# Even layer of a four-layer forward pass: products in another order, recurrence operands made chunk by chunk, key norms by token, padded exponentials

## What is computed

```python
def even_mixer(xn, ...):
    proj = xn @ w_in                                  # 256 x 1024 @ 1024 x 2816
    lru_x, lru_g, rw = jnp.split(proj, [512, 1024], axis=-1)
    h = rg_lru(causal_dwconv(lru_x, conv_w, conv_b), gate_a_w, ...)
    y_lru = jax.nn.gelu(lru_g) * h
    y_rwkv = rwkv7_mixer(rw, shift_mu, ...)
    return jnp.concatenate([y_lru, y_rwkv], axis=-1) @ w_out

def rwkv7_mixer(p, mu, w0, w2, a0, a2, g2, k_k, k_a, r_k, gn_w, gn_b):
    ps = p + (token_shift(p) - p) * mu
    r, k, v, xw, xa, xg = jnp.split(ps, idx, axis=-1)    # 512, 512, 512, 64, 64, 128
    wlog = -jax.nn.softplus(-(w0 + jnp.tanh(xw) @ w2)) - 0.5
    decay = jnp.exp(-jnp.exp(wlog))
    a = jax.nn.sigmoid(a0 + xa @ a2)
    g = jax.nn.sigmoid(xg) @ g2
    kk = hs(k * k_k)                                     # 8 heads of 64
    kk = kk / jnp.maximum(jnp.linalg.norm(kk, axis=-1, keepdims=True), 1e-12)
    k = k * (1.0 + (a - 1.0) * k_a)
    o = rwkv7_scan(r, decay, k, v, kk, a)                # recurrence over the tokens
    ...                                                  # group norm, bonus of r, k, r_k, gate g
```

## Time and profile before

| | |
|---|---|
| time, median of 3 runs | 2103.97 us (2101.36 to 2104.2) |
| the profiled execution | 2104.11 us |
| its span in the trace | 2102.0 us |
| PE / DVE / ACT / POOL busy | 92% / 75% / 55% / 3% of the span |
| mean granted clock of TensorE | 0.919 |
| DMA | 489 MB, mean 233 GB/s |
| experts (336 tiles), the largest part | DVE low splits 750.8 us, ACT high splits 625.8 us |
| low and high splits outside the experts | x100 each, 219.1 and 183.6 us |

### The profile page before, as it was taken

The page is one execution under the profiler, slowest core; times in us unless marked ns, Lnnn a source line. Parts: engine busy times, 40 slices in busy tenths (PEclk is TensorE's granted clock), DMA queues, the critical chain, the costliest instruction groups (busy, mean ns, idle before and its releaser), DMA issues.

```text
span 2102.0 us, 25666 instructions
## 1 busy us (share of the span) xinstructions
PE 1923.9 (92%) x9324; PEld 1617.9 (77%) x9324; DVE 1583.2 (75%) x1546; ACT 1152.6 (55%) x1195; POOL 59.8 (3%) x85
## 2 busy tenths in 40 slices
PE   8748979999996799999999999999999998888987
PEld 7648867778784578888888888888888877677766
DVE  6587355788867478988888988888898886656754
ACT  5411214434436466777767676776777665454542
POOL 1000000111010000000000000000000000000000
PEclk9878659999996799999999999999999999959978
DMA  7300004899640379999999999999998973313420
GB/s 260 113 1 1 31 20 160 285 326 320 208 139 35 135 278 380 332 374 349 366 346 361 378 334 371 350 363 345 359 379 335 374 273 107 119 41 113 145 81 20
DMA packets 161947, 489.02 MB, mean 233 GB/s; under 512 B 8178, under 2 KB 13427, under 8 KB 161744
## 3 DMA queue, kind: packets, MB, share of 16 engines
q1 hardware_dynamic: 153536, 458.21, 60.0%
q0 software_dynamic: 8336, 29.81, 4.0%
HBM read 485.36 MB, written 2.62 MB: 232 GB/s over the span
## 4 chain that ended last, share of the span: by engine, by line
PE 67%; DVE 14%; issue 10%; DMA 4%; ACT 4%; POOL 0%; DVEq 0%; ACTq 0%; POOLq 0%
PE bank L1127 18%; PE bank L1129 18%; PE bank L1128 18%; DVE weights_at L1819 3%; PE bank L1305 2%; DMA BIG<-in_e_ffn_down 2%; ACT weights_at L2703 1%; PE bank L1553 1%; PE bank L1278 1%; DVE BIG L2120 1%; PE bank L1618 1%; DMA BIG<-in_e_ffn_gate 1%; PE bank L1266 1%; PE bank L1293 1%; DMA BIG<-in_w_ada 1%
## 5 line engine op out<-in xcount | busy, mean ns | idle before, releaser
L2361 DVE TENSOR_TENSOR expert_weights_low<-BIG,expert_weights_high 128x2048 fp32r<-128x2048 f32 x336 | 750.8, 2288 | 58.7 <-ACT expert_weights_high L2956 58.6
L2956 ACT ACTIVATE expert_weights_high<-BIG 128x2048 fp32r<-128x2048 f32 x336 | 625.8, 1922 | 69.3 <-DMA BIG<-in_o_moe_up 38.4
L1127 PE MATMUL bank<-expert_weights_high,expert_x_high 128*128 128x512 f32 x896 | 351.8, 393 | 3.0 <-DVE expert_x_low L2426 2.9
L1129 PE MATMUL bank<-expert_weights_low,expert_x_high 128*128 128x512 f32 x896 | 349.3, 390 | 0.0
L1128 PE MATMUL bank<-expert_weights_high,expert_x_low 128*128 128x512 f32 x896 | 349.1, 390 | 0.0
L1819 DVE TENSOR_TENSOR weights_at<-BIG,weights_at 128x2048 fp32r<-128x2048 f32 (+2 forms) x100 | 219.1, 2191 | 96.3 <-ACT weights_at L2703 94.4
L2703 ACT ACTIVATE weights_at<-BIG 128x2048 fp32r<-128x2048 f32 (+2 forms) x100 | 183.6, 1836 | 177.4 <-DMA BIG<-in_e_ffn_down 39.7
L1127 PE MATMUL bank<-weights_at,x_high 128*128 128x512 f32 (+2 forms) x608 | 244.9, 403 | 25.6 <-DVE weights_at L1819 11.9
L1128 PE MATMUL bank<-weights_at,x_low 128*128 128x512 f32 (+2 forms) x608 | 239.7, 394 | 0.0
L1129 PE MATMUL bank<-weights_at,x_high 128*128 128x512 f32 (+2 forms) x608 | 239.6, 394 | 0.0
L1127 PEld LDWEIGHTS bank<-expert_weights_high,expert_x_high 128*128 128x128 f32 x896 | 168.3, 188 | 37.3 <-DVE expert_x_low L2426 3.0
(11 more groups left out here) (398 smaller groups left out, 2436.4 us busy)
## 6 DMA issues: line engine op xcount, KB each, us to landing
BIG<-in_o_moe_gate SPq DMA_DIRECT2D x112, 1024.0 KB, 5.2
BIG<-in_o_moe_up SPq DMA_DIRECT2D x112, 1024.0 KB, 5.6
BIG<-in_o_moe_down SPq DMA_DIRECT2D x112, 1024.0 KB, 5.3
BIG<-in_w_ada POOLq DMA_DIRECT2D x48, 512.0 KB, 5.0
BIG<-in_w_in SPq DMA_DIRECT2D x20, 1024.0 KB, 5.0
BIG<-in_o_w_qkv SPq DMA_DIRECT2D x12, 1024.0 KB, 5.1
BIG<-in_e_w_in SPq DMA_DIRECT2D x10, 1024.0 KB, 5.4
BIG<-in_e_ffn_gate SPq DMA_DIRECT2D x10, 1024.0 KB, 6.2
```

The lines of the kernel that those rows point to most:

```text
L1127: mm(b, high_l, high_r, start=start, stop=False, skip_group_check=not check)
L1129: last = mm(b, high_l, low_r, start=False, stop=stop, skip_group_check=not check)
L2361: tt_(E_WL[q % E_SLOTS], half(q % E_SLOTS), E_WH[q % E_SLOTS].bitcast(F32), SUB).then_inc(w_low, 1)
L2956: f(E_WH[q % E_SLOTS], half(q % E_SLOTS), ACT.Copy).then_inc(w_high, 1)
```

## The change

Six things are done at once, all in the even layer ahead of the recurrence, and nothing in the code from its end on:

- The column chunks are loaded and multiplied in the order LRU input, LRU gate, lora, k, r, v. TensorE's program is written out, with the lora products inside chunk k, g and the key sums behind r, the key norms' spread inside v, LRU gates and bonus behind v, and only the by-token groups of v ahead of the masked products; the other four stand behind these.
- The token shift is made by chunk. ScalarE empties the bank with scale 1 - mu (`unshifted`), VectorE adds mu times the bank's neighbour column (`token_shift`, 128 x 255 per block); the buffer RW is gone.
- The key norms are summed by token (matmuls of 2 columns, `key_sums`), so that root and reciprocal work on 128 x 16, and are then spread over the channels by a copy and eight matmuls with the identity (`key_norms`).
- The exponentials lie in an array with one padded column per 64 tokens (`EPP`), of which the shifted and the unshifted one are two views: two exponentials instead of three, with the factor exp(-0.5) in their scale instead of in a VectorE pass.
- Squares, the mix of keys with a and all by-token copies are ScalarE's; silu of c, exp and sin of small arrays move behind the LRU sigmoids; `lambda_difference` moves into the last step of the recurrence (c == 3), with one `low()`.
- `low()` and `high()` stand at other places and, on VectorE, in another number.

The core of the diff (left out are the plan, the semaphores, the buffers' places and the bodies that only moved):

```diff
+W_IN_ORDER = [0, 1, 5, 3, 2, 4]
...
+        EPP = R(21024, 1040).rearrange("p (c k t) -> p c k t", c=4, t=HALF + 1)
+        EP, EPX = EPP[:, :, :, 1:HALF + 1], EPP[:, :, :, 0:HALF]
...
+            w_in(0, 0)
+            w_in(0, 1)
+            w_in(1, 0)
+            w_in(1, 1)
+            w_in(5, 0)
+            w_in(5, 1)
+            w_in(3, 0)
+            loras()
+            w_in(3, 1)
+            w_in(2, 0)
+            w_in(2, 1)
+            gates_g()
+            key_sums()
+            w_in(4, 0)
+            key_norms()
+            w_in(4, 1)
+            lru_gates()
+            bonuses()
+            pe.wait_ge(shifted, 4)
+            rows_by_token((4, 5))
             pe.wait_ge(chunk_ops, 1)
...
+            rows_by_token(range(4))
...
-            gemm(6, projections, 11)
-
-            wait_taken(v, ("w_in", 9))
-            V(tt_(PS, RW[:, :, 0:T], RW[:, :, 1:T + 1], SUB))
-            for c in range(CT_RW):
-                V(stt(PS[:, c, :], PS[:, c, :], prm("e_shift_mu", c), RW[:, c, 1:T + 1], MUL, ADD),
-                  shifted if c == CT_RW - 1 else None)
+            def token_shift(c):
+                units = w_in_units(c)
+                for u in units:
+                    b = take(v, ("w_in", u))
+                    scaled_units[0] += 1
+                    v.wait_ge(shift_scaled, scaled_units[0])
+                    for i in range(2):
+                        k = 2 * u - 8 + i
+                        V(stt(PS[:, k, 1:T], b[:, i * T:(i + 1) * T - 1], prm("e_shift_mu", k), PS[:, k, 1:T], MUL, ADD),
+                          ev if i else None)
+                v.sem_inc(shifted, 1)
+            def key_inverse_norms():
+                wait_taken(v, "key_sum")
+                V(ts(s_kn, s_kn, 1e-12, None, ALU.max))
+                V(d.reciprocal(s_kn, s_kn))
+                v.wait_ge(exps_ready, 2)
+                V(d.tensor_copy(v3(KX, 16), bc(s_kn, 2, [P, 16, HALF])), key_roots)
...
+            low()
+            rotations()
+            lambdas()
+            low()
+            softplus()
+            convolution(0)
+            convolution(1)
+            low()
+            convolution(2)
+            convolution(3)
+            low()
+            token_shift(5)
+            low()
+            decay_sums()
+            low()
+            token_shift(3)
+            v.wait_ge(exps_ready, 2)
+            V(tt_(KT, PS[:, 4:8, :], KT, MUL))
+            low()
+            token_shift(2)
+            key_inverse_norms()
+            bonus_products()
+            low()
+            chunk_operands()
+            low()
+            token_shift(4)
...
-            V(ts(KN, KN, 1e-12, None, ALU.max))
-            V(d.reciprocal(KN, KN))
-            V(tt_(KK, KK, KN, MUL))
...
+                elif c == 3:
+                    lambda_difference()
+                    low()
...
+            sigmoids("lora", (TMP, KB), ("e_w0", "e_a0"))
+            high()
+            for c in range(4):
+                A(f(KT[:, c, :], KB[:, c, :], ACT.Identity, scale=prm("e_k_a", c), bias=s_omka[:, c:c + 1]))
+            high()
+            act.wait_ge(cum_ready, 1)
+            per_chunk = CW.rearrange("p c (k t) -> p c k t", t=HALF)
+            A(f(EP, per_chunk, ACT.Exp, scale=-math.exp(-0.5)), exps_ready)
+            A(f(EN, CW, ACT.Exp, scale=math.exp(-0.5)), exps_ready)
+            unshifted(3)
+            high()
```

## The result

The changed kernel takes 2143.35 us (median of 4 runs, 2143.17 to 2143.51) against 2103.77 for the kernel before in the same comparison (2101.36 to 2104.2): a ratio of 1.0184, 95% interval 1.0171 to 1.0198. Forecast were 2124 us and a range up to 2136. The direction was right; the loss is 39.6 us instead of 20. The profiled execution took 2143.31 us with a span of 2141.5.

The account below looks back on a forecast made before the run. The even layer's preparation was taken as a chain between engines, the feed-forward as TensorE-bound. 2104 - 12 (earlier recurrence) + 32 (low splits one tile behind) = 2124 us, own spread 2110 to 2134, range 2097 to 2136.

Parts of the forecast that it names:

- 130': Start of the first recurrence product in the changed kernel (the mark ' means its times), instead of 142.25: a gain of 12.
- I take 3.5 of 0 to 6: First products: us lost to TensorE's lowered clock behind three new waits, where the rule alone gave 6.9.
- the first is nearly covered by ScalarE's exponentials: First products: the clock loss behind the 5.7 us wait is hidden by ScalarE's exponentials; only 0.6 shows.
- The lag as such: Behind the preparation: 13 low splits instead of 14 put each later place one tile behind; +32 us, bounds 24 and 42.
- The output product: From VectorE's end at 320.36 to tile 20's low split: late splits make TensorE wait, +10.5 us in sum.
- TensorE waits 2.3: Output product: TensorE waits 2.3 us for tile 13's low split, which now comes there, ending at 322.7'.
- D: Feed-forward: time of down-first's load, from the end of up-first's low split to ScalarE's high split; taken as 6.0.
- The turn: Feed-forward: a turn takes 34.4 + D = 40.4 us instead of 34.8; three turns cost +11.6.
- I take 6.0, bounds 5.0 and 8.0: Feed-forward: size of D; 5.0 when nothing else loads, 7.6 with an ada load just ahead.
- the upper row (7.6): Feed-forward: the profile's load time with an ada load just ahead; by the shared-engines rule 2 us more in four turns.
- The lag is not absorbed: Rival, lag absorbed in the feed-forward's turns: faster, 2104 - 15 + 7 = 2096; chance 0.15.
- The preparation gains nothing: Rival: clock stays at half through tiles 7 to 11, 15 more; 2104 + 3 + 32 = 2139; chance 0.07.

Follow-up runs that it names:

- experiment 1: Changed kernel with low(2) in place of low() in the recurrence's last step, so 14 low splits again: 2091.02 us, ratio 0.9934.
- experiment 3: Changed kernel with modulation loads of 64 columns instead of 1024 behind the first two steps: 2123.64 us, ratio 1.0071.
- experiment 8: Changed kernel with low(2) in the recurrence's last step and modulation loads of 64 columns: 2087.15 us, ratio 0.9923.
- experiment 9: Changed kernel with one low split more at the end of the feed-forward's first chunk: 2106.55 us, ratio 1.0007.
- experiment 2: Kernel before with one low split less in the first products (10 instead of 11 in that loop): 2150.92 us, ratio 1.0213.
- experiment 4: Kernel before with one low split moved from the first products into the recurrence's last step: 2097.76 us, ratio 0.9976.

## Why the prediction was right in kind and short in size

- **The preparation.** The waits were forecast at 5.7, 7.4 and 10.8 and are 6.8, 7.2 and 11.1; the first masked product was forecast at 130' and is at 133.46. What failed is the term "I take 3.5 of 0 to 6" for the clock. Four tiles stand behind a wait and each takes 1.7 to 1.9 us more (windows above), 7.3 in all. The wait of 3.3 ahead of tile 6 was in the sum with its length (46.8 to 50.2') and not with its clock, and "the first is nearly covered by ScalarE's exponentials" was wrong: the chain of waits of the changed kernel (start, us, what) goes from tile 7's product over k's last ScalarE passes, which wait for the product and not for the exponentials, to tile 9's low split.

```profile
76.58 0.48 ACT BIG L2834
...
77.69 0.49 DVE BIG L2016
...
80.11 2.30 DVE weights_at L1890
```

The page "TensorE: Matmul & The Clock Gate" of the Trainium skill ("What's actually happening") has the throttled state as the default, from which activity releases the engine. By that rule alone three waits stood at 6.9; the trace gives these three 5.6 and the fourth 1.7, which is nearer to the rule than to my discount. The mark itself is partly scatter and partly luck. The traces of experiments 1, 3, 8 and 9, with the same code up to there, have it at 131.1 to 131.9; they reach tile 7 at 66.7 to 67.4, this one at 68.92. And behind tile 7 the changed kernel needs 64.5 us where the forecast without clock had 61.4, though the clock took 5.6 there: other steps were priced some 2.5 us too long.
- **The lag as such.** That 13 low splits instead of 14 make all later places one tile late was right: experiments 1, 2 and 4 show it twice, at 52.3 and 53.2 us (48.5 by the stages of the two traces). The forecast was 32 (24 to 42): the term was mis-sized in all its parts, and this is what put the time outside the range.
- **The output product**, 14.6 instead of 10.5: "TensorE waits 2.3", 3.1 and 2.1 were right (1.95, 3.26, 2.20), but I let the product behind a wait take 5.6 us. It takes 7.35 (313.85 to 321.20) and 7.11 (324.49 to 331.60), 3 us together, and the next split waits for the sum of both. The same clock price that I had set for the preparation was left out here. Up to down-first of chunk 1's hidden values it is 7.0 instead of 5.1: D is 7.1 there (405.28 to 412.40) instead of 6.0, the rest was not taken apart.
- **The turn**, 43.1 instead of 40.4: the chain D + 34.4 was right and D was not. "I take 6.0, bounds 5.0 and 8.0" met 8.8, 7.3 and 7.2, on average 7.8, which makes 5.3 of the 8.2 us missed in three turns. I counted one modulation load ahead of it; two steps stand there (four issues of 512 KB). I set the upper row (7.6) aside because "the engines are less full". They are less full over the three turns (a DMA share of 0.76), but it is the loads issued just ahead that count. The main page of the Trainium skill, "Trainium Kernel Development and Optimization" ("Key Constraints"), has all queues on the same 16 engines. By that rule the higher row was the one to take, and the runs agree (experiment 3: 5.1, 5.0 and 5.1 without those loads). The other 2.9 us lie in the 34.4: from down-first to up-first's low split the turns take 24.5, 25.1 and 25.0 instead of 24.4, with VectorE waiting for the down product at the lower clock and for the gate tile's late load, and behind D they take 10.4, 10.6 and 10.4 instead of 10.0.
- **The q, k, v tiles**, 7.1 instead of 4.9, were not taken apart further.
- **Rivals.** The lag is not absorbed: VectorE's idle time before low splits didn't take it up but moved. VectorE's groups show it (busy, mean ns, idle before), first those of the kernel before from 311.84 to 551.91 us, then those of the changed one from 302.87 to 588. The idle time before splits fell from 39.4 to 25.2 us, and that before the low part of the hidden values rose from 0.7 to 39.7, behind the load that had become late.

```profile
L1819 DVE TENSOR_TENSOR weights_at<-BIG,weights_at 128x2048 fp32r<-128x2048 f32 (+1 forms) x40 | 85.3, 2132 | 39.4 <-ACT weights_at L2703 38.6
...
L2135 DVE TENSOR_TENSOR hidden_low<-bank,hidden_high 128x512 fp32r<-128x512 f32 (+1 forms) x12 | 7.8, 647 | 0.7 <-ACT hidden_high L2817 0.3
```

```profile
L1890 DVE TENSOR_TENSOR weights_at<-BIG,weights_at 128x2048 fp32r<-128x2048 f32 (+1 forms) x40 | 85.3, 2132 | 25.2 <-ACT weights_at L2801 24.3
...
L2233 DVE TENSOR_TENSOR hidden_low<-bank,hidden_high 128x512 fp32r<-128x512 f32 (+1 forms) x12 | 7.8, 647 | 39.7 <-ACT hidden_high L2943 39.5
```

"The preparation gains nothing" is wrong too: the clock came back to 1.00 between the waits (74.62 to 80.30 above).

## What to carry to other kernels

Where splits or loads are handed out by a counter, count the calls ahead of each stage on every engine when code ahead of it is rewritten: one call missing in an idle place cost 52 us, spread over the 335 us behind it. Price a wait of TensorE with its length and, from a row of the same trace, with what the clock takes behind it, everywhere and not only where the clock is on one's mind; for waits under 3 us give that price as a range from nothing to the full one. For a load on the path look at what is issued in the few us ahead of it, not at the average share of the DMA engines.

## What the runs showed of the hardware

Behind a wait of 3.3 us the next 5.7 us were granted 0.70 of the clock (35 matmuls in place of 50), much as behind those of 6.8, 7.2 and 11.1 us, 1.7 to 1.9 us lost each time: in the preparation the price did not grow with the wait. Shorter waits went either way. Behind one of 1.95 us the product of 7.35 us was granted 0.77 (313.85 to 321.20 of the changed kernel), behind one of 2.94 the next was granted 1.00 (394.54 to 400.30). The same wait of 1.85 us ahead of tile 5 left the clock at 1.00 in the changed kernel (45.47) and had 0.68 behind it in experiment 9 (44.74 to 48.96).

From the issue of a load of 1 MB to the start of the split that waits for it 5.1 us passed where no large modulation load was about, and 8.8 us with four of 512 KB issued up to 3.4 us ahead of it.
